# Who turns the rows: VectorE in place of TensorE for three turns of each mixed layer

## The reference

```python
h = rms_norm(x, mix_norm[l])
aq, ak, av, bq, bk, bv, cq, ck, cv, cg, gates = jnp.split(h @ w_in[l], split_points, axis=-1)
qa = rope(_rms_f32(aq.reshape(bsz, S, A_HEADS, 2, D_HEAD), a_q_norm[l]))     # first branch
ka = rope(_rms_f32(ak.reshape(bsz, S, A_HEADS, 2, D_HEAD), a_k_norm[l]))
y_a = diff_attention(qa, ka, va, lam, lam_init, a_subln[l])
...
merged = (g[:, :, 0] * (y_a @ w_branch_a[l]) + g[:, :, 1] * (y_b @ w_branch_b[l])
          + g[:, :, 2] * (y_c @ w_branch_c[l]))
x = x + merged @ w_out[l]
x = x + 0.5 * swiglu_ffn(x, ffn2_norm[l], ffn2_w_gate[l], ffn2_w_up[l], ffn2_w_down[l])
```

## Time and profile before

| | us |
|---|---|
| median of 3 runs | 1856.77 |
| lowest and highest | 1856.0, 1857.78 |
| the profiled execution | 1856.61 |
| its span (first to last instruction) | 1854.8 |
| PE busy | 1832.9 (99%) |
| POOL, ACT, DVE busy | 1363.4 (74%), 916.2 (49%), 859.1 (46%) |
| granted TensorE clock, mean | 0.998 |

### The profile page before, as it was taken

How to read it: one execution, slowest core, us unless ns; L and a number is a source line. 1 busy time by engine, 2 the same in 40 slices (tenths; PEclk the granted TensorE clock), 3 DMA queues, 4 the chain that set the end, 5 groups by cost and what they waited for, 6 DMA issues and landing times.

```text
span 1854.8 us, 25509 instructions
## 1 busy us (share of the span) xinstructions
PE 1832.9 (99%) x9626; PEld 1509.2 (81%) x9626; DVE 859.1 (46%) x1598; ACT 916.2 (49%) x1365; POOL 1363.4 (74%) x568
## 2 busy tenths in 40 slices
PE   6999999999999999999999999999999999999999
PEld 5889887887888888888788888888888878888887
DVE  4203775776644531955651430723085565243252
ACT  3324522765454744455564544554455556545442
POOL 2624354457869798978689798969897967898885
PEclk9999999999999999999999999999999999999999
DMA  9762586648757576556456566557655645656663
GB/s 354 257 238 64 166 312 217 167 121 284 253 182 279 171 231 192 194 185 180 129 171 196 166 205 192 194 172 244 199 193 179 175 152 159 193 159 212 193 194 126
DMA packets 194842, 363.98 MB, mean 196 GB/s; under 512 B 32261, under 2 KB 48373, under 8 KB 194165
## 3 DMA queue, kind: packets, MB, share of 16 engines
q1 hardware_dynamic: 191856, 354.87, 60.4%
q10 hardware_dynamic: 2884, 7.73, 1.2%
HBM read 361.50 MB, written 6.10 MB: 198 GB/s over the span
## 4 chain that ended last, share of the span: by engine, by line
PE 97%; DMA 1%; DVE 1%; ACT 1%; issue 0%; ACTq 0%; SPq 0%
PE ps L1157 29%; PE ps L1159 28%; PE ps L1158 28%; PE ps L1374 2%; PE ps L1827 1%; PE ps L1828 1%; PE ps L1826 1%; PE ps L1202 1%; PE ps L1753 1%; PE ps L1526 1%; PE ps L1175 1%; PE ps L1497 1%; PE ps L1507 1%; PE ps L1798 1%; PE ps L1412 1%; DMA raw<-in_pool_w_in 1%
## 5 line engine op out<-in xcount | busy, mean ns | idle before, releaser
L535 POOL TENSOR_TENSOR w_lo<-raw,w_hi 128x1024 fp32r<-128x1024 f32 x556 | 1344.4, 2455 | 441.9 <-ACT w_hi L573 419.7
L573 ACT ACTIVATE w_hi<-raw 128x1024 fp32r<-128x1024 f32 x556 | 571.6, 1058 | 396.3 <-DMA raw<-in_ffn_w_up 101.1
L1157 PE MATMUL ps<-w_hi,xt_hi 128*128 128x512 f32 x1888 | 745.0, 395 | 5.8 <-DVE xt_lo L2027 4.6
L1159 PE MATMUL ps<-w_hi,xt_lo 128*128 128x512 f32 x1888 | 733.2, 388 | 0.0
L1158 PE MATMUL ps<-w_lo,xt_hi 128*128 128x512 f32 x1888 | 732.8, 388 | 0.0
L1157 PEld LDWEIGHTS ps<-w_hi,xt_hi 128*128 128x128 f32 x1888 | 355.1, 188 | 85.9 <-issue 11.8
L1159 PEld LDWEIGHTS ps<-w_hi,xt_lo 128*128 128x128 f32 x1888 | 355.1, 188 | 74.1
L1158 PEld LDWEIGHTS ps<-w_lo,xt_hi 128*128 128x128 f32 x1888 | 355.4, 188 | 68.5
L2374 DVE STREAM_TRANSPOSE ps<-proj 32x256 f32<-32x256 f32 (+1 forms) x384 | 166.6, 434 | 6.9 <-DVE xt_lo_ctx L2393 0.5
L1157 PE MATMUL ps<-w_hi,xt_hi_ctx 128*128 128x512 f32 (+1 forms) x432 | 167.4, 388 | 0.2
L1159 PE MATMUL ps<-w_hi,xt_lo_ctx 128*128 128x512 f32 (+1 forms) x432 | 166.5, 385 | 0.0
(11 more groups left out here) (232 smaller groups left out, 1593.7 us busy)
## 6 DMA issues: line engine op xcount, KB each, us to landing
raw<-in_w_in SPq DMA_DIRECT2D x120, 512.0 KB, 3.7
raw<-in_ffn_w_gate SPq DMA_DIRECT2D x88, 512.0 KB, 4.3
raw<-in_ffn_w_up SPq DMA_DIRECT2D x88, 512.0 KB, 4.4
raw<-in_ffn_w_down SPq DMA_DIRECT2D x88, 512.0 KB, 3.5
pt<-in_ada_w SPq DMA_DIRECT2D x44, 512.0 KB, 6.2
raw<-in_pool_w_in SPq DMA_DIRECT2D x32, 512.0 KB, 8.6
raw<-in_na_w_in SPq DMA_DIRECT2D x32, 512.0 KB, 5.3
raw<-in_conv_w_in SPq DMA_DIRECT2D x32, 512.0 KB, 4.8
```

The costliest lines, as they stand in the source:

```text
L535: pool.tensor_tensor(w_lo[:, s, :], raw[:, s, :], w_hi[:, s, :].bitcast(F32), ALU.subtract).then_inc(lo_done, 1)
L573: act.activation(w_hi[:, g % SLOTS, :], raw[:, g % SLOTS, :], ACT.Copy).then_inc(hi_done, 1)
L1157: pe.matmul(o, h, hi, start=start, stop=False)
L1159: return pe.matmul(o, c, hi, start=False, stop=stop)
```

## The change

- Turns 0 to 3 of keys and queries leave PE and ACT. DVE turns the keys after L2476 and the queries after the sums of block 2's squares (`heads_turned`), straight from `proj` to `qt`, 16 square instructions each. `scores(0)` waits for them. The factor 0.125 goes into the queries' rotation table, whose `tensor_tensor` (L2420) becomes a `scalar_tensor_tensor`.
- Merged turns 0 and 1 leave PE. DVE makes them in two lots of 8 instructions (`merged_turned`), one before and one after the gate product of j = 3, into the same banks 0 and 1. The low parts 0 and 1 move from behind j = 3's product to behind j = 4's.
- ACT's high parts 0 and 1 wait for DVE's turn in place of PE's. ACT's order of splits is left as it is.
- Merged turns 2 and 3 stay on PE but stand behind the third group of `mix_out` in place of the second.

```diff
-MIX_TURN_AT = {11: (0, 1), 13: (2, 3), 17: (4, 5), 19: (6, 7), 31: (8, 9)}
+MIX_TURN_AT = {17: (4, 5), 19: (6, 7), 31: (8, 9)}
...
-                    if G in (11, 13):
-                        turned(MIX_TURN_AT[G][0])
-                        turned(MIX_TURN_AT[G][1])
...
-                    act.wait_ge(pe_done, pe_s.count(("tp", f"m{l}", 0, k)))
+                    if k < 2:
+                        act.wait_ge(dve_done, dve_s.count(("tp", f"m{l}")))
+                    else:
+                        act.wait_ge(pe_done, pe_s.count(("tp", f"m{l}", 0, k)))
...
+                    if i == 0:
+                        pe.wait_ge(dve_done, dve_s.count(("heads", l, 0)))
+                        pe.wait_ge(dve_done, dve_s.count(("heads", l, 1)))
...
-                        if j == 4 and k == 0:
...
-                            turn_merged(0)
-                            turn_merged(1)
...
-                    if k == 1:
+                    if k == 2:
                         turn_merged(2)
                         turn_merged(3)
...
+                def heads_turned(n, col):
+
+                    dve.wait_ge(dve_done, dve_s.count(("rows", l, n)))
+                    squares_turned(lambda q, o: free(qt[32 * q:32 * q + 32, 0:1, 0:1], [[SEQ, 4], [P, NT], [1, 32]], 4 * (1 - n) * SEQ + o),
+                                   lambda i, o: free(proj[32 * i:32 * i + 32, 0:1], [[P, 4], [IN_COLS, NT], [1, 32]], col + o))\
+                        .then_inc(dve_done, dve_s.one(("heads", l, n)))
...
+                heads_turned(0, AK)
                 dve.wait_ge(act_done, act_s.count(("hsq", l, 1)))
...
                 squares(2)
+                heads_turned(1, AQ)
                 inverse(2)
...
+                    if j == 4:
+                        merged_low(0)
+                        merged_low(1)
                     if br:
...
+                    if j == 2:
+                        merged_turned((0, 1))
                     if j == 3:
-                        merged_low(0)
-                        merged_low(1)
+                        merged_turned((2, 3)).then_inc(dve_done, dve_s.one(("tp", f"m{l}")))
```

More of the change, by code:

```diff
@@ L948, in root @@
                                    scale=1.0 / HD).then_inc(act_done, act_s.one(("hrms", l, n)))
[L950 to L955, removed]
                 def evicted(n, how):
@@ L1733, in turn_heads @@
                     turn(f"q{l}", 0, k, lambda t, c: pj(MIX_TURNS[k][0] + c * P, P, IN_COLS, t=t),
-                         ((act_s if k < 4 else dve_s), ("qt", l, k)), bank=4 + k % 2)
+                         (dve_s, ("qt", l, k)), bank=4 + k % 2)
                 def scores(i):
-                    for k in {0: range(4), 4: range(4, 8), 8: (8, 9)}.get(i, ()):
-                        reader = act_s if k < 4 else dve_s
-                        pe.wait_ge(reader.sem, reader.count(("qt", l, k)))
+                    if i == 0:
+                        pe.wait_ge(dve_done, dve_s.count(("heads", l, 0)))
+                        pe.wait_ge(dve_done, dve_s.count(("heads", l, 1)))
+                    for k in {4: range(4, 8), 8: (8, 9)}.get(i, ()):
+                        pe.wait_ge(dve_done, dve_s.count(("qt", l, k)))
                     read_out(4)
@@ L1849, in mix @@
                         branch_group(j, k)
-                        if j == 4 and k == 0:
-                            for n in (13, 14):
-                                pe.wait_ge(acc_free[(b + n) % 2], reads(b + n))
-                            turn_merged(0)
-                            turn_merged(1)
                 go, bo = G0[f"mix_out{l}"], B0[f"mix_out{l}"]
-                read_out(0)
-                read_out(1)
+                for k in range(2):
+                    pe.wait_ge(dve_done, dve_s.count(("xt", f"m{l}", 0, k)))
                 for k in range(4):
                     s = weights(go + k)
-                    if k % 2 == 0:
+                    if k == 0:
                         pe.wait_ge(dve_done, dve_s.count(("xt", f"m{l}", 0, k // 2)))
@@ L1950, in ada_beside, with squares_turned @@
                 ada_turns(stage, n, tiles)
-            def squares_turned(to, rows):
-                for i in range(4):
+            def squares_turned(to, rows, some=range(4)):
+                for i in some:
                     for q in range(4):
@@ L2419, in mix_tables @@
                         at, src, n = ((0, 0, HD), (NT * HD, 32, 32), (NT * HD + 32, 0, 32))[j - 6]
-                        last = dve.tensor_tensor(free(qt[:, 0:1, 0:1], [[HD, NT], [1, n]], 20 * SEQ + m * 256 + at),
-                                                 free(rope[:, 0:1, 0:1, 0:1], [[HD, NT], [1, n]], at),
-                                                 free(head_gain[:, m, 0:1], [[0, NT], [1, n]], src), ALU.mult)
+                        last = dve.scalar_tensor_tensor(out=free(qt[:, 0:1, 0:1], [[HD, NT], [1, n]], 20 * SEQ + m * 256 + at),
+                                                        in0=free(rope[:, 0:1, 0:1, 0:1], [[HD, NT], [1, n]], at), scalar=(0.125, 1.0)[m],
+                                                        in1=free(head_gain[:, m, 0:1], [[0, NT], [1, n]], src), op0=ALU.mult, op1=ALU.mult)
                     last.then_inc(dve_done, dve_s.one(("head_rope", l, j)))
@@ L2679, in merged_low, with merged_turned @@
                        .then_inc(dve_done, dve_s.one(("xt", f"m{l}", 0, k)))
+                def merged_turned(some):
+                    dve.wait_ge(dve_done, dve_s.count(("merged", l, 0)))
+                    for n in (13, 14):
+                        dve.wait_ge(acc_free[(b + n) % 2], reads(b + n))
+                    return squares_turned(lambda q, n: free(ps[32 * q:32 * q + 32, MERGED_BANK[0], 0:1], [[SEQ, 4], [P, NT], [1, 32]], n),
+                                          lambda i, n: free(proj[32 * i:32 * i + 32, 0:1], [[P, 4], [IN_COLS, NT], [1, 32]], GATES + n), some)
                 for j in range(6):
```

## The result

The changed kernel takes 1879.05 us (median of 4 runs, 1877.03 to 1881.61) against 1857.0: ratio 1.0116, 95% interval 1.0101 to 1.013. The forecast had the sign and named two of the three losses, but its +4.4 us is a fifth of the measured +22, outside the range.

What follows compares the result with a forecast made beforehand. PE was taken to bound the kernel; per mixed layer -2.67 (turns) + 0.75 (block 4's banks) + 4.1 (layer's end) = +2.2, for two +4.4, giving 1861.2 us; range 1855.0 to 1864.0.

Steps and rivals of the forecast that it cites:

- What bounds the kernel: PE, busy 1832.9 of 1854.8 us: each microsecond off it is won, each wait put into it lost for good.
- What leaves PE: Three turn pairs per mixed layer leave PE, 0.79 + 0.09 = 0.88 us each: -2.67 per layer.
- G = 16: At block 4's first product PE waits for block 2's banks, freed late behind DVE's queries' turn: +0.75 us per layer.
- The end of the layer: In `last_chunks` ACT's splits and POOL's groups come late behind DVE's merged turn, so PE waits: +4.1 us per layer.
- both causes: Layer's end: splits late behind high parts 0 and 1; last two late behind 2 and 3, floor 1.8 us; together 4.1.
- 0.1 for the restart: What PE would lose in `last_chunks` on top of its wait of 4.0 us for POOL's groups.
- The question is the spare time of three supplies: Claimed that what matters is how much time freed banks, turned rows and weight groups have to spare before PE waits.
- rival 3: Square turns into SBUF wait for POOL's port: two waits of about 28 us per layer, over +100 in all; chance 0.04.
- 1: POOL catches up at the layer's end, only the floor of 1.8 to 3 us left: 1855 to 1857.5; chance 0.21.
- 2: Group count off, so no wait of 4.1 at the layer's end: 1851.5 to 1853 us; chance 0.11 with milder forms.
- 4: Low parts 0 and 1 or `merged`'s second half also late: +6 to +10 us, 1863 to 1867; chance 0.09.
- 5: The skill's rule sending 128x128 turns to TensorE when PSUM will do; in us the same as the forecast, no own chance.

Runs made afterwards that it cites:

- x7: Changed kernel with the edits of x3 and x4, and the queries' turn moved behind the instruction that frees block 2's banks; 1851.24 us, ratio 0.9964 to the kernel before.
- x13: Changed kernel's heads' part only, with the queries' turn behind the freeing of block 2's banks and both copies ahead of maps_joined(0); 1853.22 us, ratio 0.9979.
- x4: Changed kernel with ACT's order 12 splits, high parts 0 and 1, 4 splits, high parts 2 and 3, in place of 9, 5 and 2 splits; 1868.59 us.
- x10: x7 with ACT's order 12 splits, high parts 0 and 1, 2 splits, high parts 2 and 3, 2 splits; 1855.65 us, ratio 0.9994.
- x2: Only the change's merged part on the kernel before, keys and queries turned on TensorE as before; 1866.98 us, ratio 1.0046.
- x6: Changed kernel with the edits of x3 and x4 together; 1855.35 us, ratio 0.9992 to the kernel before.
- x12: x7 without the reordered copies of turns 4 and 5, so maps_joined(0) stands between them again; 1851.74 us, ratio 0.9971.
- x3: Changed kernel with DVE making both copies of turns 4 and 5 ahead of maps_joined(0); 1868.03 us, ratio 1.0051 to the kernel before.

## Why the prediction was wrong

- **What bounds the kernel** was right: each wait put into PE was lost for good, and so was each turn pair taken off it won (x7, x13).
- **What leaves PE**: right, 0.89 a pair against 0.90 measured.
- **G = 16**: right in kind, 0.5 measured for 0.75. The square turns into SBUF have a median of 436 ns where those into PSUM have 456, and 16 take 7.18 us, not 7.45. The estimate of 0.33 us per turn from the formula in the Trainium skill (VectorE: DVE Perf Modes, the TRN2 errata) is not borne out: 0.45 is.
- **The end of the layer**: right. Turn, gap, pace and the last group's time came within 0.4 us, the wait as 4.2 for 4.1. x4 takes both causes away and the wait with them, x10 shows the second alone; the first alone was not run. What failed is a term: "0.1 for the restart", where 1.4 was paid, since the clock fell to half behind the wait. x2's net loss is 4.7 a layer, for 3.2 forecast.
- **The step that failed**: "The question is the spare time of three supplies". I followed DVE as far as the freeing of block 2's banks, took "+0.75" as the whole price of the heads' part, and did not ask what DVE's next instructions would meet. The prediction knew the mechanism: it charged POOL for DVE's two additions, and its rival 3 quotes the row with 2467 ns. It asked only whether the *new* instructions would take the port, and they don't. It was the old ones behind them, moved by the change from a stretch in which POOL had run dry (from 862.70 to 864.93, and the old pair ended at 865.1) to one where it had not. This cost 7.0 a layer with the clock behind it, nearly 14 of the 22 us.
- **Rivals**: 1 is refuted by the trace (POOL did not catch up: 18.4 us for its seven groups) and 2 by the count, which held. 3 is refuted: no turn into SBUF took longer than 441 ns. 4, "more is late", had the kind right, but its two places kept their spare time; the late place was another. As to 5, turning on TensorE was the faster choice against the changed kernel and DVE is in x7: the rule that it names decides nothing by itself.
- **The range** was too narrow above, since +6 to +10 for "more is late" was drawn from the places that I had looked at. Had only "the restart" been priced as measured, the sum would have been about +7.

The sum as it should have been: per layer -2.7 (turns) + 0.5 (block 4) + 5.7 and 1.3 (second scores with what they lost to the clock, and the clock behind them) + 4.2 and 1.4 (last chunks, clock) = 10.4; twice, 20.8; and 2.3 ahead of the mixed layers by chance, less 0.7 that the second layer did better: 22.4, which is the spans' difference, 1877.2 - 1854.8.

## What to carry to other kernels

When work goes onto an engine that isn't the bound, follow that engine past the new instructions to the next thing that the bound waits for, and look at what each of its old instructions will now run beside: here small DVE instructions with two SBUF inputs were cheap only where POOL was idle or about to be. Look also at what is queued behind every wait whose releaser changes; here seven splits that had nothing to do with the turn starved POOL. And once a wait of some microseconds enters TensorE's stream, add what follows at half clock: here it made 4.9 us to 7.0.

## What the runs showed that I had not expected

- A DVE instruction on two elements lasts 1.99 us beside a running POOL instruction and 0.22 without one.
- The place of one turn in DVE's order, worth half a microsecond a layer by its own wait, is worth 4.1 us between x6 and x7 and 16.9 between x4 and x12, by phase.
- Behind waits of 4.8 us, and of three with 3.2 in all, PE worked at a granted clock of 0.50 for about 4 us; behind 0.5, and behind 1.2 in x3 and x6, it stayed at 1.00. Behind the one of 2.1 to 2.5 in the attention layer it fell in two traces of five.
- The kernel has a place where a load's landing time decides over about 2.3 us, which is more than half of the 4.4 that was forecast.
